# Loading expert weights one megabyte at a time in the order of use, in a mixture-of-experts layer on one Trainium2 core

## What is computed

```python
h = x + jnp.concatenate([att, conv_out], axis=-1) @ w_out
hn = _rms(h, norm2_g)                      # then, for each expert e and its block of tokens xe:
gu = xe @ w_gu[e] + b_gu[e]
g, u = gu[:, :D_FF], gu[:, D_FF:]
g = jnp.minimum(g, SWIGLU_LIMIT)
u = jnp.clip(u, -SWIGLU_LIMIT, SWIGLU_LIMIT)
h = (u + 1) * (g * jax.nn.sigmoid(SWIGLU_ALPHA * g))
y = h @ w_down[e] + b_down[e]              # times the token's gate, added into the token's row
```

## Time and profile before

| | before |
|---|---|
| runs, median (lowest to highest) | 1067.05 us (1066.46 to 1068.02) |
| the profiled execution, its own time | 1068.34 us |
| its span in the trace | 1066.6 us |
| moved by DMA | 420.40 MB, mean 394 GB/s |
| TensorE busy | 96% of the span |

### The profile page before, as it was taken

One profiled execution on the slowest core, in us unless ns is written; L12 is line 12 of the kernel. 1 busy time (PEld: TensorE's weight loads), 2 busy tenths in 40 slices (PEclk: granted clock), 3 DMA queues, 4 the chain that ended last, 5 costly groups with the idle time before them and its releaser, 6 DMA issues.

```text
span 1066.6 us, 11844 instructions
## 1 busy us (share of the span) xinstructions
PE 1018.7 (96%) x5105; PEld 476.6 (45%) x5106; DVE 325.5 (31%) x579; ACT 91.9 (9%) x163; POOL 7.4 (1%) x19
## 2 busy tenths in 40 slices
PE   9999999999999999989898989989898989999997
PEld 7767454444444444434343434344343434334333
DVE  4633031243323232322323241323223232413243
ACT  2222030010000000000000010000000000100001
POOL 0100000000000000000000000000000000000000
PEclk9999999999999999999999999999999999999999
DMA  9970969999999999999999999999999999999997
GB/s 346 292 210 3 383 258 395 418 419 419 413 428 426 427 427 428 429 427 428 427 429 429 428 428 428 429 427 428 430 427 429 427 429 428 428 415 420 422 416 265
DMA packets 61524, 420.40 MB, mean 394 GB/s; under 512 B 21452, under 2 KB 21776, under 8 KB 30640
## 3 DMA queue, kind: packets, MB, share of 16 engines
q1 hardware_dynamic: 61024, 419.32, 95.5%
q0 software_dynamic: 352, 0.55, 0.2%
q10 hardware_dynamic: 112, 0.03, 0.0%
HBM read 418.29 MB, written 1.58 MB: 394 GB/s over the span
## 4 chain that ended last, share of the span: by engine, by line
PE 69%; DMA 28%; SPq 2%; DVE 0%; issue 0%; POOL 0%; POOLq 0%; DVEq 0%
PE ps L956 35%; DMA ring<-in_w_gu_dram 27%; PE ps L970 6%; PE ps L871 5%; PE ps L788 5%; PE ps L996 3%; PE ps L806 3%; PE ps L659 2%; PE ps L882 2%; PE ps L981 1%; PE ps L958 1%; DMA ring<-in_w_down_dram 1%; PE ps L998 1%; SPq L544 1%; PE ps L817 1%; PE ps L621 1%
## 5 line engine op out<-in xcount | busy, mean ns | idle before, releaser
L956 PE MATMUL ps<-ring,xT 128*64 128x512 f32 x1008 | 455.3, 606 | 29.6 <-DMA ring<-in_w_gu_dram 29.4
L958 PE MATMUL ps<-ring,xT 128*64 128x512 f32 x1000 | 452.7, 606 | 0.0
L956 PEld LDWEIGHTS ps<-ring,xT 128*64 128x64 f32 x1008 | 135.6, 139 | 304.2 <-issue 300.1
L970 PE MATMUL ps<-ring,he 128*64 128x512 f32 x472 | 210.5, 595 | 9.7 <-DMA ring<-in_w_down_dram 8.8
L972 PE MATMUL ps<-ring,he 128*64 128x512 f32 x472 | 211.1, 596 | 0.0
L958 PEld LDWEIGHTS ps<-ring,xT 128*64 128x64 f32 x1000 | 134.5, 139 | 0.0
L970 PEld LDWEIGHTS ps<-ring,he 128*64 128x64 f32 x472 | 61.7, 137 | 137.3 <-issue 137.1
L1787 DVE TENSOR_TENSOR acc<-ps,acc 128x512 f32<-128x512 f32 x52 | 33.7, 687 | 185.0 <-PE ps L996 185.0
L871 PE MATMUL ps<-oh,x 128*128 128x128 f32 x512 | 68.4, 286 | 0.0
L871 PEld LDWEIGHTS ps<-oh,x 128*128 128x128 f32 x512 | 64.0, 196 | 6.4 <-issue 3.4
L1401 ACT COPY gu_sb<-ps 128x1024 f32<-128x1024 f32 x16 | 16.2, 1012 | 577.6 <-PE ps L958 577.6
(11 more groups left out here) (269 smaller groups left out, 723.6 us busy)
## 6 DMA issues: line engine op xcount, KB each, us to landing
ring<-in_w_gu_dram SPq DMA_DIRECT2D x86, 2048.0 KB, 27.0
ring<-in_w_down_dram SPq DMA_DIRECT2D x46, 2048.0 KB, 27.1
ring<-in_w_gu_dram SPq DMA_DIRECT2D x79, 1024.0 KB, 12.2
ring<-in_w_down_dram SPq DMA_DIRECT2D x26, 1024.0 KB, 12.3
ring<-in_w_down_dram SPq DMA_DIRECT2D x12, 512.0 KB, 17.9
w_chc<-in_w_in_dram SPq DMA_DIRECT2D x1, 4096.0 KB, 20.1
w_qkv<-in_w_in_dram SPq DMA_DIRECT2D x4, 768.0 KB, 8.1
w_b<-in_w_in_dram SPq DMA_DIRECT2D x1, 2048.0 KB, 27.3
```

The lines of the kernel that those rows point to most:

```text
L956: even = mm(gu_banks(j)[0:CAP, n, :], xT[j % 2][:, k, 0:CAP], first[n], start=(k == 0), stop=(k == KT - 1))
L958: odd = mm(gu_banks(j)[CAP:P, n, :], xT[j % 2][:, k, CAP:P], second[n], start=(k == 0), stop=(k == KT - 1))
L970: even = mm(out[0:CAP, half, :], hid[:, f, 0:CAP], first[2 * a + half], start=(f == 0), stop=(f == FT - 1))
```

## The change

All entries of `ORDER` are now in the order of use, and every entry is one load of 1 MB; the test that made loads of two chunks is gone. The halves and quarters at the end stay as they are, and so do the seven chunks outside the ring. Slots are still given by (n + 1) % 16. `LOADS` had 237 entries, 132 of them of two chunks; it now has 369, all of one chunk. TensorE's matmuls are the same in the same order.

```diff
                     IN_USE += [(2 * pair + s, c) for c in chunks for s in range(2)]
-                    ORDER += [(2 * pair + s, c + a) for c in chunks[::2] for s in range(2) for a in range(2)]
         ALL = len(IN_USE)
-        EARLY, FINE = 2 * 2 * GUC + 2 * DNC, 4 * GUC + 4
-        ORDER[:EARLY] = IN_USE[:EARLY]
-        ORDER[ALL - FINE:] = IN_USE[ALL - FINE:]
+        EARLY = 2 * 2 * GUC + 2 * DNC
+        ORDER += IN_USE
...
             e, c = ORDER[n]
-            two = (FIRST_TWO <= n < RINGED + 1 - FINE and c % 2 == 0 and ORDER[n + 1] == (e, c + 1)
-                   and slot_of(n) < RING - 1)
-            LOADS.append((n, 1 + two))
-            n += 1 + two
+            LOADS.append((n, 1))
+            n += 1
```

## The result

| | before | after |
|---|---|---|
| median (lowest to highest) | 1066.98 us (1066.46 to 1068.02), 4 runs | 1076.97 us (1076.15 to 1077.11), 4 runs |
| ratio, 95% interval | | 1.0089 (1.0076 to 1.0101) |
| the profiled execution, its span | 1068.34, 1066.6 us | 1076.84, 1075.1 us |

The changed kernel is slower by 10.0 us. 12.3 us were forecast, 1079.4 us within 1073.5 to 1086. The spans of the two profiled executions differ by 8.5 us, since the one before was 1.4 us longer than its median and the one after 0.1 us shorter.

The account below looks back on a forecast made before the run. The DMA stream of bytes was taken to bound the kernel, with TensorE's spare time off the path. The median of 1067.05 us plus 12.3 us for slower single loads, all else nothing, gave 1079.4 us, within 1073.5 to 1086.

Parts of the forecast that it names:

- What bounds the kernel: Whole stream: DMA engines busy throughout; a late pair's 25.17 MB at 428 GB/s take 58.8 us, TensorE needs 52.7.
- What the change adds: The 264 single loads run at 420 GB/s instead of 428: 659.1 us against 646.8, 12.3 us more.
- Evidence from what TensorE did: With TensorE 100% busy either way, two-chunk loads ran at 426 and 429 GB/s, single ones at 418 and 422.
- What the change takes away, at nothing: Shorter single waits of TensorE and earlier slot refills save nothing; its waiting grows 1.1 us per pair.
- SyncE's queue: 24 issues per pair instead of 12; long issues, median 2.13 us, come from a full queue, covered by 26.4 us queued.
- The end: Last 36 entries, halves and quarters, unchanged; the end shifts with the stream, nothing added or saved.
- no change: Stretches at 418 and 420 GB/s are slow for their own reasons; the middle keeps 428, time 1067 us; 6%.
- Faster, by gaps in the stream: Small stream gaps put TensorE's waits on the path; late pairs start 2.45 us earlier, 23 us less, 1044 us; 3%.
- SyncE setting the pace: SyncE's issue of single loads at 2.68 us each limits the stream: 61 us, giving 1128 us; 3%.
- TensorE's clock: More frequent waits lower TensorE's clock; at 0.87 some ten pairs lose 19 us, giving 1098 us; 3%.
- The two figures of the Trainium skill: Fixed 2.0 us per DMA would cost 264 us, judged not paid; 32 bytes per descriptor, 0.2%, about 1.3 us.

## Why the prediction was right, point by point

- **What bounds the kernel**: right. The period of a late pair went with the rate of its bytes, and 39 us of work added to TensorE changed nothing. (The first flat slices are 418, 419, 419 and 413, not only 418 to 419; nothing rests on it.)
- **What the change adds**: the mechanism was right and the size 2.3 us too large. The term was 264 chunks at 420 GB/s against 428. In periods the two rates are 25.17 MB / 59.66 us = 421.8 and 25.17 / 58.76 = 428.3 GB/s, which gives 9.9 us. I chose the value of a stretch of 50 us printed as 420; the same stretch of the changed kernel shows 421. The prediction allowed 1.5 us for rounding, and at a difference of 7 in 428 a unit of rounding is a seventh of the answer. The distance of two pieces of the chain is the finer ruler, but before the change TensorE was busy throughout in both stretches of single loads, so their periods were those of its work and not of the bytes.
- **Evidence from what TensorE did**: right, and now shown. With the work added to TensorE it was busy 548 of 560 us, where it had been busy 525, and the rate stayed at 428 GB/s; in the changed kernel with the same work it was busy 544 and the rate was 422.

```profile
330.00:890.00 560.00, 543.66 (x2879) 1.00 1.01 422
```

- **What the change takes away, at nothing**: right. The stretch of 560 us holds 9.5 pairs before and 9.4 after, so the waits for loads went from 3.6 to 4.7 us a pair, 1.1 more as forecast.
- **SyncE's queue**: right. From 330 to 890 us an issue took a median of 2.13 us, up to 6.3, with the DMA share at 1.01: the issues were long, and the engines never ran dry. SyncE also waited 213.4 us of the 560 for free slots. That the cause of the long issues is a full queue isn't shown (last section).

```profile
L461 SPq DMA_DIRECT2D ring<-in_w_gu_dram x156: 327/2132/6304, 329.8 to 884.1; - x156
DMA to landing us min/median/max: 14.6/27.0/29.9
...
SPq L461 <- PE ps L954: 156.8, 69, 6.4
SPq L461 <- PE ps L968: 56.6, 39, 5.3
```

- **The end**: right that the whole shifts with the stream: 9.4 us from the last landing to the end against 9.3. The place of the last landing was read wrongly. The prediction has the stream end at about 1054 us, some 12 us before the end; by the chain the last load landed at 1057.3. The sum doesn't use it.
- **The rivals**: no change fell with the rate of 421. Faster, by gaps in the stream: there were none, and shorter waits brought nothing. SyncE setting the pace: the share stayed at 1.01 and SyncE had 213 us of waits to spare. TensorE's clock: it went the other way, from 0.98 to 1.00.
- **The two figures of the Trainium skill** ("DMA: Bandwidth & Descriptors"): the fixed 2.0 us for each DMA, which the section "Anatomy of one DMA — SWDGE (gpsimd) path" fits to transfers issued from GpSimd, isn't paid in this stream, for 264 loads and 132 of twice the size gave the same time. The 32 bytes for each descriptor in the section "Why small descriptors are slow (HBM only)" would be 0.2%; the rate of the pairs fell by 1.5%. The same section has a second term that the prediction left out, some 3 cycles for each packet, beside 256 cycles for 8 KB at 32 bytes each. From 16 to 8 KB that would be 0.6% more (an estimate from that page). Both together are about half of what was measured, some 9 ns for each row and engine; the measurement decides.

## What to carry to other kernels

Where the DMA engines are busy throughout, count rows (contiguous pieces per partition), not loads: here each costs an engine 9 ns, 3% of an 8 KB row, and joining two neighbours in HBM saves one of the two, while joining two that aren't neighbours doesn't. What still longer rows could give is small: by 9.3 ns for each of the 96 rows of a pair, rows of 16 KB still cost 0.9 us of its 58.76 (an estimate from the three periods). Joining isn't free at the point where the queue is shallow: compare the pause that a load of two slots adds with the time from issue to landing there. And a busy share of 96% says little: a few microseconds of idle engine per period, ended by loads, with a period equal to bytes over rate, mean that the loads set the time.

## What the runs showed that I had not expected

**The clock went with the length of single waits, not with their sum.** In the kernel before, TensorE waited 2.7 us for a load five times between 330 and 890 us, and after each of the five the granted clock of the next 5 us was 0.66. After its three waits of 1.6 us it was 1.00. One stretch of each kind:

```profile
812.00:817.00 5.00, 4.01 (x12) 0.66 0.99 423
646.00:651.00 5.00, 4.47 (x22) 1.00 1.01 429
```

The changed kernel waited longer in sum, 44.1 us, but at most 1.3 us at once, and its stretch shows 1.00; with rows of 4 KB the sum was 55.4 us, the longest wait 1.5, and the clock 1.00 too. With single loads in the old order, and waits of up to 3.0 us, the mean clock of the execution was 0.991, as in the kernel before (0.990), and it was 0.999 in the changed one.

It isn't a rule of waits alone. The kernel with loads of two until 20 entries from the end waited 2.7 us at 753.5 us, and the 20 us around it show 1.00. And with the work added to TensorE in the kernel before, the clock fell once while TensorE had been busy for over 10 us:

```profile
945.00:950.00 5.00, 5.00 (x20) 0.99 1.00 419
950.00:955.00 5.00, 5.00 (x34) 0.66 1.02 431
```

Whether the finer order would gain by its clock in a kernel bound by TensorE, no run here shows; here it is spare time.

**Fewer megabytes under way with shorter rows.** With rows of 4 KB the median landing in the late stretch was 18.6 us at 2.56 us per MB, some 7.3 MB under way. With rows of 8 KB and the same ring it was 27.0 us at 2.49 us per MB, some 10.9 MB. SyncE's issue took 2.36 and 2.13 us in the median. The kernel before had as much under way, 27.1 us at 2.45 us per MB, some 11.1 MB in rows of 16 KB, and its issues took 0.375 us. So it isn't the megabytes under way that make an issue long. In rows the three are some 710 of 16 KB, 1390 of 8 KB and 1860 of 4 KB (estimates from these times). Long issues come with many rows, but a queue that holds one fixed number of rows would have held as many in the second as in the third. What sets the limit stays open.

```profile
L472 SPq DMA_DIRECT2D ring<-in_w_gu_dram x147: 472/2358/5361, 329.7 to 888.0; - x147
DMA to landing us min/median/max: 16.9/18.6/21.8
```
